# Late modulation columns summed on VectorE during the convolutions; decay weights in 33 small items with four buffers

## The chip, the cores and the metric

The kernel runs on one core of a Trainium2 chip. The metric is device time of one execution in microseconds; the kernel before has a median of 1655.15 over three runs (1654.78 to 1664.68). In this text PE is TensorE, PEld its weight load, DVE is VectorE, ACT is ScalarE, POOL is GpSimd and SP is SyncE.

## The reference, cut to what matters

One layer of a two-stream block in fp32: 1024 latent tokens and 256 context tokens, 1024 features. It modulates the inputs with columns computed from `c`, projects them to q, k, v, gates and decay rates, runs two linear-attention mixers, and ends with a projection and an MLP. These lines bear on the change:

```python
mod_x = (silu_c @ w_ada[l] + b_ada[l])[:, None, :]          # 6 * 1024 columns; shift/scale 1 are needed at once,
sh1x, sc1x, gt1x, sh2x, sc2x, gt2x = jnp.split(mod_x, 6, axis=-1)   # the other four parts only after the mixers
hx = rmsnorm(x, norm1_g[l]) * (1.0 + sc1x) + sh1x
p = h @ w_in                                                 # q_a, k_a, v_a, g_a, r_a, qkv_b, g_b, ...
lr = jnp.einsum('btr,zrk->zbtk', r_a, w_lr) + b_lr[:, None, None, :]
gla_log_a = (jax.nn.log_sigmoid(lr.astype(f32)) / GLA_TAU)   # summed along 64-token chunks, then exp
qkv = jax.nn.silu(short_conv(qkv_b, conv_w, rows)).astype(f32)
ya = rmsnorm(o_gla, gla_norm_g) * jax.nn.silu(p['gla_g'])    # the gates
```

## The kernel before, in words

The program is a row of phases: modulate (to 62 us), project (62 to 541 us), mix, merge and MLP. The change is in `project_phase` alone. Each engine there runs an instruction list of its own, written out in one fixed order, and waits on semaphores; nothing is planned at run time.

**Units and outputs.** `UNITS` lists 15 column groups of `w_in`, 256 columns each but for the first. Each is loaded by SP (`load_unit`), rounded by ACT and completed by DVE (`split`, lines 758 and 917: high and low part). PE forms each output as 8 x 3 matmuls (`mm3`, lines 80 to 82) in one of three PSUM buffers of `ps_main`; it may start output i only when ACT has copied out output i - 3 (`main_out`). All engines walk the same list `outs`:

- 3 small outputs, then 32 outputs of the convolution units k, k, v, v, q, q: two tiles per unit, each of three outputs (512, 512 and 256 tokens) for k and v, two for q. ACT copies them to the single buffer `u_sb`; after the last one DVE does the convolution (`conv`, lines 929 to 938), ACT the silu and the square, PE the sums of squares (`sums`, line 1157) one tile later, DVE the norm (955). PE also transposes k and v two tiles back (1176), and DVE copies that out (`turn_out`, 974), the first two groups before its convolution.
- 10 outputs ka and qa (ACT puts them into `qk`), 20 outputs va and 32 gate outputs. For these ACT copies each to `t_sb` (879), gates through Silu, and POOL (SP for the last unit) stores it.

**Decay rates.** Twelve outputs of kind `lr` stand in the same list, four behind qa, four in the first va unit, four at the end of the second: one small matmul (1191), then on ACT a copy and Abs, Exp, Ln (844 to 851), on DVE a min-and-subtract (1070), and after each four the running sums (`decay_sums`, scans of line 1006).

**Decay weights.** 17 items (`ITEMS`), four token tiles each (two for the context): DVE forms differences (`weight_sums`, 1017 or 1024 to 1027), ACT the exponential (`weight_exp`, 801 to 807), DVE multiplies by q or k (`weigh`, 1038), SP stores (`store_item`, 642). `SUMS_AT` and `WEIGH_AT` put an item's differences at one output and its product at the next, with the exponential at the first of the two; there are two buffers. 9 items start in the va outputs, 8 in the gate outputs. The Silu of the gates and the Exp of the items are in different function tables, so ACT loads a table at each turn (lines 750 and 879).

**Late modulation columns.** The four parts of `mod_x` that are needed later (32 groups of 128 columns) are made during the 32 gate outputs, one group behind each: SP loads 512 KB of `w_ada` (617), PE multiplies by silu(c) (`late_columns`, 1111), DVE copies the row out (`late_out`, 962), PE turns it into a column (`late_turn`, 1117).

## Time and profile before

| | us |
|---|---|
| median of three runs (lowest, highest) | 1655.15 (1654.78, 1664.68) |
| the profiled execution, its own time | 1664.6 |
| its span | 1662.8 |
| PE busy / DVE busy / ACT busy in the span | 1517.3 / 946.6 / 745.6 |
| mean granted TensorE clock | 0.961 |

The page cuts the span into 40 slices of 41.6 us. The phase that is changed covers slices 2 to 13:

```profile
PE   7699999998899697787888997899999999999997
DVE  4345451475540245555557439455555599988875
ACT  6446253546541444435434215455555554333333
PEclk9699999998999899999899999999999999999999
DMA  9313332355984466656614311244445586454322
```

A digit is a busy share in tenths (9 is 90% or more); PEclk is the clock that TensorE was granted, in tenths of full speed. A busy PE is not PE at its peak, since matmuls overlap and their ends are modelled: the distance from one start to the next says more than a duration.

### The profile page before, as it was taken

The numbers are of one execution on the slowest core, as the hardware profiler recorded it, in microseconds if no ns is written. First come the engines' busy times: TensorE is split into PE (matmuls) and PEld (weight loads), VectorE is DVE, ScalarE is ACT, GpSimd is POOL, SyncE is SP. The second block draws the span as 40 slices with busy tenths as digits, with TensorE's granted clock in tenths as the row PEclk, the third lists the DMA queues.
The fourth block names the chain that finished last, engine by engine and source line by source line (L and its number), as shares of the span: only waits on it lengthen the run. The fifth ranks groups of instructions, "written<-read, shape, count | busy, mean of one in ns | idle before, by whom it ended". The sixth has DMA issues, their size and how long they took to land. (4 is left out here: it accounts for less than half of the span.)

```text
span 1662.8 us, 33993 instructions
## 1 busy us (share of the span) xinstructions
PE 1517.3 (91%) x14508; PEld 1284.8 (77%) x14508; DVE 946.6 (57%) x1330; ACT 745.6 (45%) x1249; POOL 265.5 (16%) x237
## 2 busy tenths in 40 slices
PE   7699999998899697787888997899999999999997
PEld 6488878786798687776777886788888878888885
DVE  4345451475540245555557439455555599988875
ACT  6446253546541444435434215455555554333333
POOL 0001110011110132233223104132222200000000
PEclk9699999998999899999899999999999999999999
DMA  9313332355984466656614311244445586454322
GB/s 325 84 62 107 89 112 63 111 178 162 290 262 143 126 209 188 196 172 206 182 52 164 115 64 63 96 139 142 156 160 164 177 310 253 141 183 161 123 89 102
DMA packets 195736, 254.44 MB, mean 153 GB/s; under 512 B 34525, under 2 KB 127201, under 8 KB 195586
## 3 DMA queue, kind: packets, MB, share of 16 engines
q1 hardware_dynamic: 190002, 234.31, 43.4%
q0 software_dynamic: 5584, 17.95, 3.4%
q8 instruction: 116, 1.90, 0.5%
q14 instruction: 34, 0.28, 0.1%
HBM read 178.17 MB, written 74.05 MB: 152 GB/s over the span
## 5 line engine op out<-in xcount | busy, mean ns | idle before, releaser
L87 PE MATMUL fps<-xh_m,w1r_hi 128*128 128x512 f32 x448 | 176.6, 394 | 11.9 <-ACT s L2562 3.1
L88 PE MATMUL fps<-xl_m,w1r_hi 128*128 128x512 f32 x448 | 175.5, 392 | 0.0
L89 PE MATMUL fps<-xh_m,w1r_lo 128*128 128x512 f32 x448 | 175.3, 391 | 0.0
L87 PE MATMUL fps<-bh,ah 128*128 128x512 f32 x448 | 174.4, 389 | 0.4 <-DVE acc L2891 0.4
L88 PE MATMUL fps<-bl,ah 128*128 128x512 f32 x448 | 174.3, 389 | 0.0
L89 PE MATMUL fps<-bh,al 128*128 128x512 f32 x448 | 174.3, 389 | 0.0
L80 PE MATMUL ps_main<-whi,hhi 128*128 128x256 f32 x416 | 126.8, 305 | 6.5 <-ACT t_sb L879 4.0
L2534 ACT ACTIVATE ah<-araw 128x2048 fp32r<-128x2048 f32 x28 | 53.8, 1921 | 162.6 <-PE fps L89 133.6
L80 PE MATMUL ps_main<-hhi,whi 128*128 128x512 f32 (+1 forms) x336 | 125.6, 374 | 0.0
L81 PE MATMUL ps_main<-wlo,hhi 128*128 128x256 f32 x416 | 122.8, 295 | 0.0
L82 PE MATMUL ps_main<-whi,hlo 128*128 128x256 f32 x416 | 122.7, 295 | 0.0
L82 PE MATMUL ps_main<-hhi,wlo 128*128 128x512 f32 (+1 forms) x336 | 122.5, 364 | 0.0
L81 PE MATMUL ps_main<-hlo,whi 128*128 128x512 f32 (+1 forms) x336 | 122.4, 364 | 0.0
L87 PEld LDWEIGHTS fps<-xh_m,w1r_hi 128*128 128x128 f32 x448 | 84.7, 189 | 31.8 <-issue 8.6
L89 PEld LDWEIGHTS fps<-xh_m,w1r_lo 128*128 128x128 f32 x448 | 84.8, 189 | 17.8
L87 PEld LDWEIGHTS fps<-bh,ah 128*128 128x128 f32 x448 | 84.1, 188 | 18.8 <-issue 1.2
L88 PEld LDWEIGHTS fps<-xl_m,w1r_hi 128*128 128x128 f32 x448 | 85.0, 190 | 17.6
L89 PEld LDWEIGHTS fps<-bh,al 128*128 128x128 f32 x448 | 84.1, 188 | 17.5
L88 PEld LDWEIGHTS fps<-bl,ah 128*128 128x128 f32 x448 | 84.1, 188 | 17.3
L2736 DVE TENSOR_TENSOR w1r_lo<-w1raw,w1r_hi 128x512 fp32r<-128x512 f32 x96 | 75.9, 792 | 36.7 <-ACT w1r_hi L2525 36.7
L80 PEld LDWEIGHTS ps_main<-whi,hhi 128*128 128x128 f32 x416 | 85.1, 205 | 11.6 <-issue 11.6
L81 PEld LDWEIGHTS ps_main<-wlo,hhi 128*128 128x128 f32 x416 | 85.2, 205 | 0.0
(325 smaller groups left out, 3301.0 us busy)
## 6 DMA issues: line engine op xcount, KB each, us to landing
s_hid<-hb SPq DMA_DIRECT2D x112, 256.0 KB, 2.3
araw<-s_hid SPq DMA_DIRECT2D x28, 1024.0 KB, 5.6
room<-in_w_ada SPq DMA_DIRECT2D x32, 512.0 KB, 4.9
w1raw<-in_w_ff SPq DMA_DIRECT2D x16, 1024.0 KB, 5.7
w2b<-in_w_ff SPq DMA_DIRECT2D x16, 1024.0 KB, 9.8
raw<-in_w_in SPq DMA_DIRECT2D x14, 1024.0 KB, 5.3
s_wl<-room SPq DMA_DIRECT2D x24, 512.0 KB, 4.6
wl<-s_wl SPq DMA_DIRECT2D x16, 768.0 KB, 7.2
```

The costliest lines, as they stand in the source:

```text
L80: pe.matmul(out, lhi, rhi, start=start, stop=False)
L81: pe.matmul(out, lhi, rlo, start=False, stop=False)
L82: return pe.matmul(out, llo, rhi, start=False, stop=stop)
L87: pe.matmul(out, lhi, rhi, start=start, stop=False, skip_group_check=True)
L88: pe.matmul(out, lhi, rlo, start=False, stop=False, skip_group_check=True)
L89: return pe.matmul(out, llo, rhi, start=False, stop=stop, skip_group_check=True)
L2534: act.activation(flat(a_hi[v][:]), flat(araw[n % 2][:]), ACT.Copy).then_inc(a_hi_done, 1)
L2736: dve.tensor_tensor(w1r_lo[:, i], weight(n), w1r_hi[:, i].bitcast(F32), ALU.subtract).then_inc(w_lo, 1)
```

## The change

- The late columns leave the gate outputs and PE. `late_sum` on DVE multiplies and adds the eight 128-column pieces of a group (two `tensor_scalar`, six `scalar_tensor_tensor`, one addition), one group behind each of the 32 convolution outputs. `late_turn` stays on PE, as one matmul per group, against a column of ones; PE does them in batches ahead of `sums`, three groups behind. The loads of `w_ada` go to two buffers during the convolutions, issued by SP between the unit loads.
- The 12 rates are no outputs any more. They come two at a time behind the last three ka outputs and the first three qa outputs, in `ps_sq`, context first; Abs and the min read PSUM, so that the copy to `lr_x` is gone.
- The decay weights are 33 items of two token tiles: three around qa, then one at every 1.6 outputs of va and gate. Three buffers serve the first twelve, four the rest. Differences are at output n, the exponential at n + 1, and the product at the next item's start, behind its differences.
- Running sums of both halves of the latent tokens now have room at once (`cs_of`).

```diff
-        LRSEG = (0, 2, 1)
+        LRSEG = (2, 0, 1)
...
-        cs_lat, cs_ctx = room[:, 5120:7200], m.sb("cs_ctx", [P, 1040])[:]
-        slots = [room[:, 7200 + 2048 * i:9248 + 2048 * i] for i in range(2)]
+        cs_ctx = m.sb("cs_ctx", [P, 1040])[:]
+        cs_of = [room[:, 5120:7200], room[:, 7200:9280], cs_ctx]
...
+        slots = [room[:, 9280:10304], room[:, 10304:11328], lr_flat, room[:, 0:1024]]
...
+        NROW, LAG = 6, 3
+        arow = t_sb[:, 0:3].rearrange("p x (y n) -> p (x y) n", n=P)
+        brow = t_sb[:, 3].rearrange("p (x n) -> p x n", n=P)
+        late = [cs_ctx[:, :KT * P], lr_flat]
...
-                        if kind == "qa":
-                            outs.append((u, "lr", 2 * j + s, 0))
...
-                    if u == VA and t < 4:
-                        outs.append((u, "lr", 4 + t, 0))
-                    if u == VA + 1 and t >= 6:
-                        outs.append((u, "lr", 2 + t, 0))
...
-        PART = ((0, 4), (4, 4), (8, 2))
+        PART = ((0, 2), (2, 2), (4, 2), (6, 2), (8, 2))
+        CTX = 4
         KIN, QIN = LEVELS, LEVELS + 1
-        KINDS = [KIN, QIN] + list(range(LEVELS))
-        ITEMS = [(0, kind) for kind in KINDS] + [(2, KIN)] + [(1, kind) for kind in KINDS]
-        def place(n):
-
-            if n < 2 * NT:
-                return VA + n // NT, n % NT
-            return VA + 2 + (n - 2 * NT) // TL, (n - 2 * NT) % TL
-
-        starts = [1 + 2 * i for i in range(9)] + [20 + 2 * i for i in range(8)]
-        SUMS_AT = {place(n): i for i, n in enumerate(starts)}
-        WEIGH_AT = {place(n + 1): i for i, n in enumerate(starts)}
+        REST = [QIN] + list(range(LEVELS))
+        ITEMS = ([(CTX, KIN), (0, KIN), (1, KIN)] + [(x, kind) for x in (0, 1) for kind in REST]
+                 + [(x, kind) for x in (2, 3) for kind in [KIN] + REST])
+        SLOT = [i % 3 if i < 12 else i % 4 for i in range(len(ITEMS))]
+        uses = lambda i: SLOT[:i].count(SLOT[i])
+
+        def tick(u, kind, j, s):
+
+            if kind in ("ka", "qa"):
+                return 3 * j + s if kind == "ka" else 6 + 2 * j + s
+            if kind in ("va", "gate"):
+                return 10 + NT * (u - VA) + j if kind == "va" else 10 + 2 * NT + TL * (u - VA - 2) + j
+            return -1
+
+        starts = [6, 7, 8] + [10 + 8 * i // 5 for i in range(len(ITEMS) - 3)]
+        SUMS_AT = {n: i for i, n in enumerate(starts)}
+        EXP_AT = {n + 1: i for i, n in enumerate(starts)}
+        weighed = [n for n in starts[1:]] + [starts[-1] + 2]
+        conv_outs = [i for i, o in enumerate(outs) if o[1] in ("k", "v", "q")]
+        LATE_AT = {i: g for g, i in enumerate(conv_outs)}
+        GATE0 = 10 + 2 * NT
+
+        def rates_at(n):
+
+            return (2 * n - 6, 2 * n - 5) if 3 <= n < 9 else ()
...
             def load_late(g):
-                if g < NL:
-                    sp.wait_ge(wt_done, 8 if g < 2 else 9)
-                    sp.wait_ge(st_qk, 16)
-                else:
+                if g >= NL:
                     sp.wait_ge(ar_ready, g - NL + 1)
                 c0 = LATE0 + g * P
-                sp.dma_start(late[g % NL].rearrange("p (k n) -> p k n", n=P), av[:, :, c0:c0 + P]).then_inc(ld_a[g % NL], 16)
+                sp.dma_start(late[g % NL].rearrange("p (k n) -> p k n", n=P), av[:, :, c0:c0 + P]).then_inc(ld_a[g % 4], 16)
...
+            load_late(0)
+            load_late(1)
+            load_unit(3)
+            g = 2
+            for u in range(4, VA + 1):
                 load_unit(u)
-                if u == NU - 3:
-                    for i in range(4):
-                        store_item(i)
-                if u == NU - 2:
-                    for i in range(4, 8):
-                        store_item(i)
-                    load_late(0)
-                    load_late(1)
-                    store_item(8)
-                    load_late(2)
-            for g in range(NL, NLATE):
-                load_late(g)
-                if g % 2 == 0 and 9 <= 7 + g // 2 < len(ITEMS):
-                    store_item(7 + g // 2)
-                if g - 4 >= NLATE - TL:
-                    store_gate(g - 4 - NLATE + TL)
-            for t in range(TL - 4, TL):
+                upto = min(sum(o[0] <= u - 3 for o in outs) - 3 + NL, NLATE) if u < VA else NLATE
+                for g in range(g, upto):
+                    load_late(g)
+                g = upto
+            load_unit(VA + 1)
+            load_unit(VA + 2)
+            done = 0
+            for u, upto in ((VA + 3, 10), (VA + 4, 10 + NT), (VA + 5, GATE0)):
+                done = store_items(done, upto)
+                load_unit(u)
+            for t in range(TL):
+                done = store_items(done, GATE0 + 3 * TL + t)
                 store_gate(t)
+            for i in range(done, len(ITEMS)):
+                store_item(i)
             for i in range(4):
                 sp.wait_ge(st_g[i], 32)
-            for i in range(2):
-                sp.wait_ge(st_w[i], 32 * ((len(ITEMS) + 1 - i) // 2))
+            for i in range(4):
+                sp.wait_ge(st_w[i], 32 * SLOT.count(i))
...
+            def rates(j):
+                n, b = SEG[LRSEG[j // 4]][1], j % 2
+                log_exp()
+                if j == 0:
+                    act.wait_ge(ar_ready, NLATE)
+                act.wait_ge(lr_ready, j + 1)
+                if j >= 2:
+                    act.wait_ge(lr_done, j - 1)
+                act.activation(lr_e[:, b, :n], ps_sq[:, j % 3, :n], ACT.Abs).then_inc(lr_abs, 1)
+                act.wait_ge(lr_abs, j + 1)
+                act.activation(lr_e[:, b, :n], lr_e[:, b, :n], ACT.Exp, scale=-1.0).then_inc(lr_exp, 1)
+                act.wait_ge(lr_exp, j + 1)
+                act.activation(lr_e[:, b, :n], lr_e[:, b, :n], ACT.Ln, bias=1.0).then_inc(lr_ln, 1)
...
+                n = tick(u, kind, j, s)
+                for x in rates_at(n):
+                    rates(x)
+                if n in EXP_AT:
+                    weight_exp(EXP_AT[n])
...
-            def late_out(g):
-                dve.wait_ge(ar_ready, g + 1)
-                if g >= 2:
-                    dve.wait_ge(sel_done, g - 1)
-                dve.tensor_copy(arow[:, g % 2], ps_sq[:, 2 * (g % 2), :P]).then_inc(ar_out, 1)
+            def late_sum(g):
+                a, b, step = arow[:, g % NROW], brow[:, g % 2], ar_step[g % 2]
+                w = late[g % NL].rearrange("p (k n) -> p k n", n=P)
+                before = 8 * (g // 2)
+                dve.wait_ge(ld_a[g % 4], 16 * (g // 4 + 1))
+                if g >= NROW:
+                    dve.wait_ge(sel_done, g - NROW + 1)
+                for k in range(KT):
+                    to, c = (a, b)[k % 2], K.csil[:, k, 0:1]
+                    if k < 2:
+                        dve.tensor_scalar(to, w[:, k], c, None, ALU.mult).then_inc(step, 1)
+                    else:
+                        dve.wait_ge(step, before + k - 1)
+                        dve.scalar_tensor_tensor(to, w[:, k], c, to, ALU.mult, ALU.add).then_inc(step, 1)
+                dve.wait_ge(step, before + KT)
+                dve.tensor_tensor(a, a, b, ALU.add).then_inc(ar_ready, 1)
+
+            def late_kept():
+                dve.wait_ge(sel_done, NLATE)
+                dve.tensor_copy(K.mod[:, 32:40, 1], K.cols[:, 56:64])
+                dve.tensor_tensor(K.mod[:, 16:48, 0], ps_sq[:, 2, 256:256 + NLATE], K.cols[:, 16:48], ALU.add).then_inc(mod_done, 1)
...
+                n = tick(u, kind, j, s)
+                if n == 3:
+                    late_kept()
+                for x in rates_at(n):
+                    rates(x)
+                if n in SUMS_AT:
+                    weight_sums(SUMS_AT[n])
+                    if SUMS_AT[n]:
+                        weigh(SUMS_AT[n] - 1)
+                if i in LATE_AT:
+                    late_sum(LATE_AT[i])
                 if u >= 1 and i + 1 == out_by[u - 1] + 1 and u + 1 < NU:
                     split(u + 1)
-            dve.wait_ge(sel_done, NLATE)
-            dve.tensor_copy(K.mod[:, 32:40, 1], K.cols[:, 56:64])
-            dve.tensor_tensor(K.mod[:, 16:48, 0], ps_sq[:, 1, :NLATE], K.cols[:, 16:48], ALU.add)
+            weigh(len(ITEMS) - 1)
...
-            def late_columns(g):
-
-                pe.wait_ge(ld_a[g % NL], 16 * (g // NL + 1))
-                if g == 0:
+            def rates(j):
+                if j == 0:
+                    pe.wait_ge(rt_out, 3)
+                    pe.wait_ge(ld_s, 64)
                     pe.wait_ge(lnss_done, 8)
-                if g >= 2:
-                    pe.wait_ge(ar_out, g - 1)
-                w = late[g % NL].rearrange("p (k n) -> p k n", n=P)
-                for k in range(KT):
-                    q = slice(32 * (k % 4), 32 * (k % 4) + 32)
-                    last = pe.matmul(ps_sq[q, 2 * (g % 2), :P], K.csil[:, k, :], w[:, k, :], start=(k < 4), stop=(k >= 4))
-                last.then_inc(ar_ready, 1)
+                if j >= 3:
+                    pe.wait_ge(lr_done, j - 2)
+                if j == 0:
+                    late_turns(NLATE)
+                if j == 2:
+                    pe.wait_ge(mod_done, 1)
+                t0, n = SEG[LRSEG[j // 4]]
+                pe.matmul(ps_sq[:, j % 3, :n], wlr[:, j % 4 * P:(j % 4 + 1) * P], raT[0:RANK + 1, t0:t0 + n], start=True,
+                          stop=True).then_inc(lr_ready, 1)
 
             def late_turn(g):
 
-                pe.wait_ge(ar_out, g + 1)
-                pe.matmul(ps_sq[:, 1, g:g + 1], arow[:, g % 2], K.sel[:, 8:9], start=True, stop=True).then_inc(sel_done, 1)
+                pe.wait_ge(ar_ready, g + 1)
+                pe.matmul(ps_sq[:, 2, 256 + g:257 + g], arow[:, g % NROW], K.ones[:, 0:1], start=True, stop=True).then_inc(sel_done, 1)
+
+            turned = [0]
+
+            def late_turns(upto):
+
+                for g in range(turned[0], upto):
+                    late_turn(g)
+                turned[0] = max(turned[0], upto)
...
-                    if kind == "gate":
-                        g = (u - NU + 4) * TL + j
-                        late_columns(g)
-                        if g:
-                            late_turn(g - 1)
...
+                        if n_norm(cn - 1):
+                            pe.wait_ge(lnss_done, n_norm(cn - 1))
+                        late_turns(LATE_AT[i] - LAG + 1 if i in LATE_AT else NLATE - 1)
                         sums(cn - 1)
                     if kind in ("k", "v", "q") and s >= last_s - 1:
                         turn(cn - 2, (0, 1) if s < last_s else (2,))
-            late_turn(NLATE - 1)
+                    for x in rates_at(tick(u, kind, j, s)):
+                        rates(x)
```

## Rows read from the trace of the kernel before

**Rows 1.** four stages of the phase: start:end, then per engine busy us and count, clock, DMA

```profile
78.70:255.90 177.20, 177.20 (x897) 146.72 (x895) 83.30 (x111) 84.04 (x91) 21.40 (x26) 1.00 0.31 95
255.90:314.50 58.60, 58.11 (x267) 44.76 (x265) 12.21 (x15) 27.50 (x35) 2.17 (x3) 1.00 0.18 54
314.50:397.50 83.00, 73.88 (x501) 67.72 (x500) 55.36 (x100) 41.82 (x73) 12.12 (x22) 0.90 0.61 196
397.50:538.00 140.50, 128.24 (x1333) 117.33 (x1336) 56.48 (x88) 57.91 (x70) 13.55 (x25) 0.95 0.70 215
```

**Rows 2.** waits in the va stage: us in total, times, longest

```profile
ACT room L801 <- DVE room L1027: 28.7, 6, 6.2
PE ps_main L80 <- ACT t_sb L879: 4.0, 3, 2.9
```

**Rows 3.** PE timeline after such a wait: start us, duration us, engine, line, operation

```profile
328.67 0.41 PE L82 MATMUL ps_main<-whi,hlo 128*128 128x256 f32 x1
328.88 0.41 PE L80 MATMUL ps_main<-whi,hhi 128*128 128x256 f32 x1
```

**Rows 4.** PE timeline, first matmuls of two va outputs, then round one gate output

```profile
340.18 0.28 PE L80 MATMUL ps_main<-whi,hhi 128*128 128x256 f32 x1
343.06 0.28 PE L80 MATMUL ps_main<-whi,hhi 128*128 128x256 f32 x1
480.02 0.65 PE L1111 MATMUL ps_sq<-room,csil 128*32 128x128 f32 x16
480.59 0.38 PE L1117 MATMUL ps_sq<-sel,lr_x 128*128 128x1 f32 x2
480.84 0.36 PE L80 MATMUL ps_main<-whi,hhi 128*128 128x256 f32 x1
483.87 0.64 PE L1111 MATMUL ps_sq<-room,csil 128*32 128x128 f32 x16
```

**Rows 5.** PE's waits in the gate stage

```profile
PE ps_sq L1117 <- DVE lr_x L962: 8.8, 3, 3.9
PE ps_sq L1111 <- DMA room<-in_w_ada: 3.5, 1, 3.5
```

**Rows 6.** ACT timeline in the gate stage: one table turn, and an exponential of 1024

```profile
438.06 0.39 ACT L879 ACTIVATE t_sb<-ps_main 128x256 f32<-128x256 f32 x1 [2.40 <-PE ps_main L82]
438.47 1.28 ACT L750 ACT_TABLE_LOAD   x1
439.77 1.92 ACT L801 ACTIVATE room<-room 128x2048 f32<-128x2048 f32 x1
441.70 1.28 ACT L879 ACT_TABLE_LOAD   x1
408.52 1.06 ACT L806 ACTIVATE room<-room 128x1024 f32<-128x1024 f32 x1 [0.97 <-DVE room L1017]
```

**Rows 7.** groups by line and shape, PE: busy us, mean ns, idle before

```profile
L1191 PE MATMUL ps_main<-raT,wlr 17*128 17x512 f32 x16 | 8.9, 636 | 2.6 <-ACT t_sb L879 2.6
L1191 PE MATMUL ps_main<-raT,wlr 17*128 17x256 f32 x8 | 3.0, 452 | 0.0
```

**Rows 8.** DVE: four scalar_tensor_tensor of 128 columns in a row, and their group

```profile
572.16 1.12 DVE L1600 SCALAR_TENSOR_TENSOR rr<-pr,gt,vtn 128x128 f32<-128x128 f32 x4 [1.77 <-PE pr L1759]
L1600 DVE SCALAR_TENSOR_TENSOR rr<-pr,gt,vtn 128x128 f32<-128x128 f32 x80 | 22.5, 344 | 17.3 <-PE pr L1759 16.7 <-ACT vtn L1485 0.5
```

**Rows 9.** DVE timeline, one v tile of the convolutions

```profile
172.19 1.29 DVE L974 COPY room<-ps_tr 128x512 f32<-128x512 f32 x2 [4.97 <-PE ps_tr L1176]
175.85 0.89 DVE L929 TENSOR_SCALAR room<-room,cols 128x1280 f32<-128x1280 f32 x1 [2.37 <-ACT room L857]
180.30 0.42 DVE L974 COPY room<-ps_tr 128x256 f32<-128x256 f32 x1
190.71 0.89 DVE L929 TENSOR_SCALAR room<-room,cols 128x1280 f32<-128x1280 f32 x1 [2.37 <-ACT room L857]
```

**Rows 10.** the late columns' loads (line 617), issue to landing

```profile
DMA to landing us min/median/max: 3.8/4.9/9.7
```

More of the change, by code:

```diff
@@ L585, in item @@
             t0, n = PART[part]
-            return t0, n, kind, slots[i % 2][:, :512 * n], (cs_ctx if part == 2 else cs_lat), 4 * n
+            cs = cs_of[2 if part == CTX else part // 2]
+            off, z = (0, 8 * PW) if part == CTX else (8 * PW * (part % 2), 16 * PW)
+            return t0, n, kind, slots[SLOT[i]], cs, off, z
         def view(t, off, dims):
@@ L997, in _ @@
             last.then_inc(ab_kept, 1)
-            def decay_sums(part):
-                cs = cs_ctx if part == 2 else cs_lat
-                if part == 0:
-                    dve.wait_ge(init_done, 4)
-                dve.wait_ge(lr_done, (4, 12, 8)[part])
-                for x in range(4 * PART[part][1]):
-                    at = slice(2 * PW * x, 2 * PW * (x + 1))
-                    last = dve.tensor_tensor_scan(cs[:, at], restart[:], cs[:, at], 0.0, ALU.mult, ALU.add)
-                last.then_inc(cs_done, 1)
@@ new lines, in weight_sums @@
+            def weight_sums(i):
+                t0, n, kind, w, cs, off, z = item(i)
+                if uses(i):
+                    dve.wait_ge(st_w[SLOT[i]], 32 * uses(i))
+                elif SLOT[i] == 2:
+                    dve.wait_ge(lr_done, 12)
+                elif SLOT[i] == 3:
+                    dve.wait_ge(wt_done, 10)
+                    dve.wait_ge(st_qk, 16)
+                dve.wait_ge(cs_done, 1 if i == 0 else 2 if ITEMS[i][0] < 2 else 3)
+                ahead, past, half_ = off, off + z, 8 * C
@@ L1185, in _ @@
                     pe.wait_ge(main_out, i - 2)
-                if kind == "lr":
-                    if j == 0:
-                        pe.wait_ge(rt_out, 3)
-                        pe.wait_ge(ld_s, 64)
-                    t0, n = SEG[LRSEG[j // 4]]
-                    pe.matmul(ps_main[:, i % 3, :n], wlr[:, j % 4 * P:(j % 4 + 1) * P], raT[0:RANK + 1, t0:t0 + n], start=True,
-                              stop=True).then_inc(main_ready, 1)
-                elif kind == "small":
+                if kind == "small":
                     t0, n = SEG[s]
```

143 lines of the change are left out of this document (62 added, 81 removed).

## The prediction, made blind

> **What bounds the kernel now.** I first read the slices of the page for where PE is not full, then the busy time of four stages of the project phase, then each stage's waits, and last the timelines of single outputs. The stages are the 32 convolution outputs, ka and qa, va, and the gates [rows 1]; together 459.3 us. In the first two PE is full (177.2 of 177.2 and 58.1 of 58.6) at full clock, while DVE and ACT have half their time free (83.3 and 84.0 of 177.2). The other two are not full, and they hold work that isn't the projection. A va output that meets no wait takes 2.88 us from its first matmul to the next output's (340.18 to 343.06) [rows 4], so 20 could take 57.6, but the stage takes 83.0 [rows 1]. The reader should see why in the waits: ACT waits six times for DVE's differences, 28.7 us in all, since differences, exponential and product of an item follow one another, and what PE needs, ACT's copy of its PSUM buffer, stands behind the exponential; PE's own longest wait on it is 2.9 us [rows 2]. Behind such a wait a 256-column matmul comes every 0.21 us (328.67 to 328.88) and not every 0.12 (2.88 over 24): the granted clock of the stage is 0.90, a mixture of the levels 2.4 and 1.2 GHz, and here PE had stood idle just before it fell [rows 1, 3]. So a wait costs more than its length.
>
> A gate output takes 3.85 us (480.02 to 483.87) [rows 4], 32 of them 123, and the stage 140.5 [rows 1]; the rest is the start of the late columns, where PE waits 8.8 us for DVE and 3.5 for a load [rows 5], with the lower clock behind it. In the 3.85 us the projection has 2.88. The columns' sixteen half-matmuls go from 480.02 to 480.59, the turn from 480.59 to 480.84, and the remaining 0.15 is lost at the changes between them.
>
> **The change, part by part.** All is counted on PE, since PE sets the time of all four stages.
>
> *Gates.* Columns and turns leave: 32 x 2.88 = 92.2. What must hold is that ACT keeps up. A gate output with an item costs ACT a copy 0.41 (438.06 to 438.47), a table load 1.30 (438.47 to 439.77), an exponential of 1024 elements, 1.06 and a little more before a table load, 1.08, and a load back, 1.30: 4.09 us [rows 6]. An output without one costs 0.41. Items come every 1.6 outputs, 18 exponentials in the first 28 gate outputs, and three weight splits of the length of a 2048-element pass, 1.92 [rows 6]: 18 x 4.09 + 10 x 0.41 + 3 x 1.92 = 83.5 us of ACT against 28 x 2.88 = 80.6 of PE. ACT is the longer by 2.9, but it may lag two outputs behind (three PSUM buffers, 5.8 us), and the last four outputs have no item. Following lag by lag through the outputs, PE stops only round the second split, where two exponentials stand at neighbouring outputs: about 2 us in all. I take 92.2 + 2.0 + 0.3 at the end = 94.5, against 140.5. The bounds are 92.2 and, if ACT had no slack at all, 92.2 + 2.9 plus a fallen clock, some 100. The same elements go through DVE as before in twice as many instructions; its 56.5 us in this stage [rows 1] leave room for that, and since its differences now stand ahead of the product of the item before, ACT's input is ready when ACT comes. A store has half the bytes and four buffers, about 6.4 outputs or 18 us for differences, exponential, product and store. SP no longer waits for columns, so its stores go out as products finish. POOL's queue is unchanged.
>
> *va.* Twelve exponentials of half the size without table loads in 20 outputs, again a step behind the differences, and no rates on ACT: PE's waits and its low clock should go. 20 x 2.88 = 57.6, and 1.4 for the row transposes and changes: 59.0 against 83.0. The three buffers give 4.8 outputs, 13.8 us, for a cycle. DVE enters va late, since the last rates' running sums stand in front; I allow 1.5 us.
>
> *ka and qa.* Twelve rate matmuls instead of four stand here. For 512 tokens one costs 8.9 / 8 = 1.11 us, for 256 it costs 3.0 / 4 = 0.75 [rows 7]. Four of 512 move in, and four of 256: 7.4 us, 66.0 against 58.6. ACT has 27.5 of 58.6 busy [rows 1] and takes on eight more rates without their PSUM copy, spread two to an output of 5 us; nothing is late there by my count. The moved rates are also what va no longer carries.
>
> *Convolutions.* PE gets the 32 turns, 0.25 us each [rows 4]: 8.0 us on an engine without a gap. DVE gets 32 sums. Four `scalar_tensor_tensor` of 128 columns take 1.12 us, so one start follows the last by (1.12 - 0.344) / 3 = 0.26 [rows 8]; every sum step waits only for the step before the last, which 0.26 hides. One group is 8 x 0.26, the tail of the last 0.08, and an addition of at most 0.34: 2.5 us, 80 in all, on 83.3 busy of 177.2 [rows 1]. That fits in the sum, but the order decides: after its convolution DVE must do three sums before the next one, and there are two buffers. The third sum can only start when the buffer of the first has been read and loaded again, median 4.9 us from issue to landing [rows 10]. For a v tile: convolution and last copy 175.85 to 180.72 = 4.87, first sum 2.5, landing 4.9 (the second sum and at times a split lie beside it), third sum 2.5, the copy of the transposes 1.29 [rows 9, 10]: 16.06 us. PE's tile is 190.71 - 175.85 = 14.86, set by PE as DVE's wait of 2.37 shows [rows 9], and 15.61 with three turns. DVE is 0.45 late per tile; in k tiles both engines have more to do, and I count them alike: 8 x 0.45 = 3.6, of which the slack of the PSUM buffers eats a little: 3 us. The q tiles have two sums for two buffers and nothing to wait for. Bounds of a landing are 3.8 and 9.7 [rows 10]: at 3.8 no loss, at 9.7 8 x 5.25 = 42. I take the median, since most of the 32 lie near it and this stage has a DMA share of 0.31 against 0.70 where they were measured [rows 1]. SP issues some of these loads behind a unit load that waits for a split; by my count those have 8 us. Sum: 177.2 + 8.0 + 3.0 = 188.2.
>
> By the rows a next small DVE operation starts before the one in front has ended, 0.26 after its start against a duration of 0.344 [rows 8]. The Trainium skill ("VectorE: DVE Perf Modes", section "The DRAIN you can't avoid") says that the next operation does not start until the pipeline is empty; by that a group would be 8 x 0.344 + 0.34 = 3.1 us, a v tile 17.2, and the stage would lose 13 us and not 3. The row decides against it here.
>
> **The sum.** 188.2 + 66.0 + 59.0 + 94.5 + 1.5 = 409.2 against 459.3: 50 us less. The profiled execution was 1664.6 and would be 1614.6. The median of the three runs lies 9.5 below it, and I take the same 50 off: 1605.
>
> **The rivals.**
>
> *B, loads late in the convolutions.* DVE becomes the bound of eight tiles. For it: the cycle above is already even with PE's at the median landing. Against it: the free DMA queues [rows 1]. At a landing of 7.5 us a tile is 18.7, 3.1 too long, 24 us in all: 1605 + 21 = 1626.
>
> *C, ACT out of time in the gates.* For it: 83.5 against 80.6, and 18 turns of the tables where there were 8. If ACT had to wait for the differences of each item, four operations of some 0.35, it would lose 1.4 x 18 = 25 us: 1630. Against it: the differences no longer wait for ACT.
>
> *D, slower.* If landings are near the longest seen, 9.7, PE stops 5.25 us in each of eight tiles, and, as in va, runs at half clock behind each stop: an output's worth of time, 2.88, is lost again [rows 3, 4, 10]. 8 x (5.25 + 2.88) = 65 against a gain of 53 without convolution waits: 1655 + 12 = 1667. It decides from a landing of about 8.2 us on.
>
> *E, a table turn that costs twice.* If each load held ACT for 2.6 us and not 1.3, 36 loads would add 47 us to ACT in the gates: no gain there, 1650. For it stands nothing in the rows: copy and exponential start 1.30 after the load's start [rows 6]. The Trainium skill ("ScalarE: Activation LUTs", section "What ACT_TABLE_LOAD costs") gives 1283 ns and a drain of 1380 ns behind it for every switch; the first agrees with 1.28 here, the second is not seen.
>
> **How the numbers follow.** The forecast has a chance of 0.63, B 0.17, C 0.13, D 0.04, E 0.03. Within 1% (16.6 us) is what a measurement of this kernel cannot tell from no change. The forecast is all faster; of B, C and E 0.06 lie within 1%; D is 0.04: faster 0.90, same 0.06, slower 0.04. The best case has no waits at all and turns at half price in a batch: 50 + 3 + 2 + 1.5 + 4 = 60 less, 1595. Upwards the range takes in B and C at their prices and a little of both: 1633. Outside are D, E and the tail of B with C.
>
> **What would show it.** Gate outputs 2.88 us apart and a gate stage of 94 to 96; va near 59 at full clock; 4.1 us of ACT for a gate copy with its item; sums of 2.5 us on DVE; convolutions near 188, with PE's waits there under 5 us in all. If the convolutions take 200 or more, the landings were mis-sized; if gates take over 100 with PE waiting on the copy to `t_sb`, ACT was; if va keeps a clock of 0.9, the waits have only moved.

## The result and the profile after

The changed kernel has a median of 1608.97 us over four runs (1606.56 to 1618.1), beside 1656.1 over four of the kernel before: a ratio of 0.9715, with an interval of 0.9664 to 0.9766. A second series gave 0.9721 (0.9697 to 0.9745). The prediction was 1605, 50 us less than before; measured are 47 less (1656.1 to 1608.97). The profiled execution took 1618.1 with a span of 1616.3, where 1614.6 was forecast for it. The mean granted clock went from 0.961 to 0.970, PE's busy time from 1517.3 to 1478.0, DVE's from 946.6 to 1016.5.

The four stages of the phase, after, cut at the same outputs as in [rows 1] (start:end, length, then busy us and count of PE, PE's weight loads, DVE, ACT and POOL, the granted clock, the DMA share and GB/s):

```profile
78.50:272.30 193.80, 186.72 (x953) 155.16 (x952) 152.96 (x391) 84.69 (x91) 21.34 (x26) 0.98 0.61 173
272.30:336.90 64.60, 64.60 (x289) 48.58 (x287) 33.13 (x80) 39.65 (x61) 1.97 (x3) 1.00 0.18 57
336.90:394.90 58.00, 58.00 (x486) 58.00 (x486) 42.17 (x95) 25.55 (x49) 12.53 (x22) 1.00 0.70 235
394.90:487.20 92.30, 92.27 (x769) 92.07 (x768) 48.75 (x77) 83.61 (x94) 13.43 (x25) 1.00 0.49 167
```

Read down the lengths: va and gates are now full and at full clock, 25.0 and 48.2 us shorter than in [rows 1]; ka and qa, which now hold all twelve rates, are 6.0 longer; the convolutions are 16.6 longer, and they are the one stage where PE isn't full (186.72 of 193.80) and the clock not 1.00. Together 408.7 against 459.3: 50.6 less. Each gate output starts 2.88 us after the one before; first matmuls of two neighbours in the timeline of PE:

```profile
394.85 0.28 PE L80 MATMUL ps_main<-whi,hhi 128*128 128x256 f32 x1
397.73 0.28 PE L80 MATMUL ps_main<-whi,hhi 128*128 128x256 f32 x1
```

What is lost in the convolutions is in the waits. First PE's, then two of DVE's, of the convolution stage after (us in total, times, longest):

```profile
PE ps_tr L1229 <- DVE room L1014: 7.1, 4, 3.8
```

```profile
DVE t_sb L992 <- DMA cs_ctx<-in_w_ada: 15.6, 7, 5.1
DVE t_sb L992 <- DMA lr_e<-in_w_ada: 2.7, 2, 2.4
```

PE waits four times for DVE's copy of the transposes, and DVE nine times for a late load. Both ends of the link can be seen on DVE's timeline round one tile (start, duration, engine, line, operation, count; in brackets the idle time before and its releaser):

```profile
133.97 0.47 DVE L992 TENSOR_SCALAR t_sb<-cs_ctx,csil 128x128 f32<-128x128 f32 x2
134.35 1.66 DVE L995 SCALAR_TENSOR_TENSOR t_sb<-cs_ctx,csil,t_sb 128x128 f32<-128x128 f32 x6
136.05 0.29 DVE L997 TENSOR_TENSOR t_sb<-t_sb 128x128 f32<-128x128 f32 x1
136.26 0.47 DVE L992 TENSOR_SCALAR t_sb<-lr_e,csil 128x128 f32<-128x128 f32 x2
...
143.51 0.48 DVE L992 TENSOR_SCALAR t_sb<-cs_ctx,csil 128x128 f32<-128x128 f32 x2 [4.88 <-DMA cs_ctx<-in_w_ada]
...
145.81 0.68 DVE L1014 COPY room<-ps_tr 128x512 f32<-128x512 f32 x1
```

A group takes 136.26 - 133.97 = 2.29 us. Two follow each other, then the third has to wait 4.88 us for the buffer that the first had read until about 136.0, and behind the third stands the copy of the transposes that PE needs. Where the next tile is late as well, PE stops, and runs at half clock for a while. PE's timeline at its longest stop:

```profile
185.05 0.66 PE L1229 MATMUL ps_tr<-ident,room 128*128 128x128 f32 x2 [3.76 <-DVE room L1014]
...
186.79 0.63 PE L80 MATMUL ps_main<-hhi,whi 128*128 128x512 f32 x1
187.22 0.63 PE L81 MATMUL ps_main<-hlo,whi 128*128 128x512 f32 x1
...
190.48 0.40 PE L80 MATMUL ps_main<-hhi,whi 128*128 128x512 f32 x1
190.71 0.40 PE L81 MATMUL ps_main<-hlo,whi 128*128 128x512 f32 x1
```

After the stop a 512-column matmul comes every 0.43 us, the spacing of the lower of the clock's two levels (1.2 GHz), and every 0.23, that of 2.4 GHz, again from 190.5 on; the whole output took 7.85 where one of its kind takes 5.55. The page gives the median from issue to landing of the two buffers' loads (512 KB each):

```profile
cs_ctx<-in_w_ada SPq DMA_DIRECT2D x16, 512.0 KB, 5.9
lr_e<-in_w_ada SPq DMA_DIRECT2D x16, 512.0 KB, 5.5
```

### The profile page after: what moved, and what is told of

Read it like the earlier page. It is cut to its first block and busy times, and to the rows that moved or that the text cites. A ratio compares the mean times of both kernels' runs of the same rounds, so it can differ in the third digit from the quotient of the medians.

```text
span 1616.3 us, 33365 instructions
## 1 busy us (share of the span) xinstructions
PE 1478.0 (91%) x13996; PEld 1259.6 (78%) x13996; DVE 1016.5 (63%) x1654; ACT 766.6 (47%) x1277; POOL 265.7 (16%) x237
## 5 line engine op out<-in xcount | busy, mean ns | idle before, releaser
L80 PE MATMUL ps_main<-whi,hhi 128*128 128x256 f32 x416 | 117.9, 284 | 0.0
L81 PE MATMUL ps_main<-wlo,hhi 128*128 128x256 f32 x416 | 117.8, 283 | 0.0
L82 PE MATMUL ps_main<-whi,hlo 128*128 128x256 f32 x416 | 117.8, 283 | 0.0
L1624 DVE COPY_PREDICATED gdn_zz<-lev_m,pd 128x256 f32<-128x256 uint32 x120 | 47.4, 441 | 63.7 <-PE pd L1794 60.8
L2936 DVE TENSOR_TENSOR acc<-acc,fps 128x1024 f32<-128x1024 f32 x54 | 64.7, 1218 | 29.1 <-PE fps L89 29.1
```

The costliest lines, as they stand in the source:

```text
L80: pe.matmul(out, lhi, rhi, start=start, stop=False)
L81: pe.matmul(out, lhi, rlo, start=False, stop=False)
L82: return pe.matmul(out, llo, rhi, start=False, stop=stop)
L1624: dve.copy_predicated(zz[:, lev, b], lev_m[:, b, lev].bitcast(mybir.dt.uint32).unsqueeze(1).broadcast_to([P, NH, C]), cells(pd[b])).then_i ...
L2936: dve.tensor_tensor(to, to, got, ALU.add).then_inc(o_out, 1)
```

## The experiments

The theory was: the gain is two changes that work on different stages, the late columns' move (convolutions and gates) and the small items (va and gates, and ka and qa by the rates); what the convolutions lose beyond the turns is the landing of the loads with only two buffers; and the items need both their number of buffers and their order. The rivals: one of the two parts brings all of it; the convolutions lose by DVE's amount of work, whatever the buffers; three buffers, or the order, would have done nothing.

### late_only: the late columns' move alone

The kernel before with the sums on DVE in the convolutions, and the loads with them. Items, rates and their order stay.

```diff
-                if kind == "gate":
-                    late_out((u - NU + 4) * TL + j)
+                if i in LATE_AT:
+                    late_sum(LATE_AT[i])
```

> The kernel before with one half of the change: late columns summed on VectorE during the convolutions, rates and the 17 large decay items as before. My theory (the two halves act on different stages, and large items in step still bind): convolutions as in the changed kernel, 194 us; ka and qa 59; va 83 as before; gates 100 to 105, since an item's chain of differences 2.4, exponential 1.95 and product 2.2 is 6.6 us where two gate outputs take 5.8. Sum 438, 21 us under the kernel before: about 1635. Rival 1 (the late columns were all there was to gain, small items add nothing): about 1609, gates at 92. Rival 2 (the items bind the gates, taking columns off TensorE only uncovers them): gates stay above 125, the time is that of before or worse.

Measured: 1657.25 (ratio 0.9974, 0.9951 to 0.9997), where I had expected 1635. The gates:

```profile
415.26:525.34 110.08, 97.44 (x769) 96.35 (x768) 48.86 (x59) 56.87 (x69) 13.44 (x25) 0.95 0.39 128
```

PE's largest wait from va on, and ACT's:

```profile
PE ps_main L80 <- ACT t_sb L887: 16.5, 9, 4.9
ACT room L805 <- DVE room L1046: 41.0, 12, 6.1
```

The gates go from 140.5 to 110.1 and not to 92, nor to the 100 to 105 on record: with the columns gone, PE meets what stood behind them, ACT's copy behind exponentials of 2048 elements that wait for their differences. The convolutions take 194.1, as in the full change, va 82.9, as before. The phase gains 13.7 us and the median only 3.6; what the profiles say of the rest is below.

### items_only: the small items alone

The changed kernel with the late columns put back behind the gate outputs on PE, in two buffers; the items take three instead of four, since the fourth is now a late buffer. This half holds four things at once: small items, the step between differences and exponential, the third buffer, and the rates' move out of va.

```diff
-        late = [cs_ctx[:, :KT * P], lr_flat]
+        late = [room[:, :KT * P], cs_ctx[:, :KT * P]]
...
-                if i in LATE_AT:
-                    late_sum(LATE_AT[i])
+                if kind == "gate":
+                    late_out((u - NU + 4) * TL + j)
```

> The changed kernel with the other half alone: the late columns go back to TensorE, one group behind each gate output (two load buffers, the decay items keep three). My theory: convolutions 177, ka and qa 64 to 65, va 58 at full clock, gates 32 x 3.85 = 123 and a few us at the start: 425, 34 us under the kernel before, about 1622. With late_only's 21 the two gains would add to 55, a little above the 47 measured together. Rival (small items cost VectorE and ScalarE so much that they only pay when TensorE does not wait on VectorE for the columns): va above 65 or gates above 135, time above 1640.

Measured: 1666.46 (ratio 1.0042, 1.0026 to 1.0059). 1622 was expected. Convolutions 177.1 and va 58.0: va's 25 us come from this half of the change alone. How much of them is the items and how much the eight rates that left va was not separated; the rates' matmuls cost ka and qa 6.0 us where they went, and in va PE had also waited 5.1 us round them (2.6 before a rate's matmul, 2.5 for a rate's copy). But the gates grew to 159.2. PE's waits in the gates:

```profile
PE ps_sq L1147 <- DMA room<-in_w_ada: 13.0, 5, 4.0
PE ps_sq L1147 <- DMA cs_ctx<-in_w_ada: 11.2, 3, 5.6
```

The timeline before the longest of them tells why the load is late (a store of an item is at L656, a late load at L631):

```profile
445.61 0.64 PE L1147 MATMUL ps_sq<-cs_ctx,csil 128*32 128x128 f32 x16
449.76 0.88 SPq L656 DMA_DIRECT2D s_wl<-lr_e  x2
450.69 0.55 SPq L631 DMA_DIRECT2D cs_ctx<-in_w_ada  x1
458.98 1.08 PE L1147 MATMUL ps_sq<-cs_ctx,csil 128*32 128x128 f32 x16 [5.59 <-DMA cs_ctx<-in_w_ada]
```

PE had read `cs_ctx` by 446.3, but its next load was issued at 450.69 only, right behind a store that had to wait until DVE had its product at 449.74. A store of a product that isn't ready stands ahead of a load whose buffer is free. So this kernel shows the items' effect on va cleanly, and on the gates only together with a worse queue.

### items_three: the same with a third late buffer, loads ahead of stores

```diff
-        late = [room[:, :KT * P], cs_ctx[:, :KT * P]]
+        late = [room[:, :KT * P], cs_ctx[:, :KT * P], room[:, KT * P:2 * KT * P]]
```

In SP's list a late load now stands ahead of the stores of its output.

> items_only with a third load buffer for the late columns in the gates, and with each load issued ahead of the stores of decay items on SyncE's queue. Theory (items_only's gates, 159 us and not 126, come from loads issued late behind a store that waits for its product, 24 us of waits for loads with half clock behind each): gates 124 to 130, project phase 32 us under the kernel before, time about 1632; then the two halves of the change add up. Rival (the loads are late because the small stores fill the queues): gates above 145, time above 1650.

Measured: 1638.98 (ratio 0.9882, 0.9861 to 0.9904), gates 133.3. The third late buffer and the loads' place in the queue gave 159.2 - 133.3 = 25.9 us together; which of the two gave how much was not tested. The 124 to 130 on record were too low: the gates still miss the 32 x 3.85 = 123 of the rows by 10, of which 8.2 are two waits for a load. (The items have three buffers here and not four; three_three shows that this costs nothing where the late columns are in the convolutions, and it was not tried here.) The items' half is thus worth 26.3 us in the phase (459.3 to 433.0), the late columns alone 13.7, both 50.6. The whole is 10.6 more than its parts. A likely reason is that the move takes PE's work from the gates, but the gates can use that only when ACT no longer stands in the way, as it does in late_only.

### late_three: a third buffer for the late loads

```diff
-        late = [cs_ctx[:, :KT * P], lr_flat]
+        late = [cs_ctx[:, :KT * P], lr_flat, K.gt2[:]]
```

`K.gt2` is memory that only the later phases write; the sums are the same work in the same places.

> The changed kernel with a third load buffer for the late columns (in a tensor that is unused during the convolutions). Theory (the four stops of TensorE in the convolutions, 7.1 us, and one output at half clock behind the longest, 2.3 us, come from VectorE waiting for the load of the third sum of a tile): VectorE's 18 us of waits for these loads nearly vanish, convolutions 184 to 186 instead of 194, 8 to 9 us less than the changed kernel in the same call. Rival (VectorE's own work, with sums of 2.3 us, is what fills a tile): waits for transposes' copies stay, time as the changed kernel.

Measured: 1601.19 (1598.32 to 1604.53), ratio 0.9645 (0.9620 to 0.9669), below the changed kernel's 0.9721 (0.9697 to 0.9745). The convolution stage, and DVE's only wait for a late load in it:

```profile
76.20:259.90 183.70, 183.46 (x955) 153.23 (x953) 152.73 (x391) 84.64 (x91) 21.35 (x26) 1.00 0.65 183
```

```profile
DVE t_sb L992 <- DMA gt<-in_w_ada: 0.5, 1, 0.5
```

193.8 became 183.7 with the same 153 us on DVE: the loss of 10.1 was the landing, not the amount of work. What is left over 177.2 is 6.5 us; PE has 0.24 us of waits in the stage, so nearly all of it is the 32 turns, at 0.20 each. The other stages are unchanged (64.6, 58.0, 92.2).

### late_one: a single buffer

```diff
-        late = [cs_ctx[:, :KT * P], lr_flat]
+        late = [cs_ctx[:, :KT * P]]
...
-            load_late(1)
             load_unit(3)
-            g = 2
+            g = 1
```

> The changed kernel with one load buffer for the late columns instead of two: each sum's load can only start when the sum before it has ended. This is case D of the prediction, made to happen. With landings of 5.9 us, two of three in a tile lie bare on VectorE: 6.2 + 3 x 2.3 + 2 x 5.9 = 24.9 us for a v tile, 26.3 for a k tile, where TensorE needs 15.5 and 17.7; q tiles 16 against 13. Theory 1 (VectorE is then the bound, and TensorE's half clock behind each stop is hidden in the next wait): convolutions 177 + 4 x 9.4 + 4 x 8.6 + 4 x 3 = 261, time about 1677. Theory 2 (as the prediction priced D, the half clock adds some 2.9 us at each of eight tiles): 284, time about 1700. Rival (the loads hide anyway): 194.

Measured: 1691.29 (ratio 1.0188, 1.0135 to 1.0242): 1.9% slower than before. The convolutions:

```profile
77.76:342.32 264.56, 201.86 (x954) 165.16 (x953) 147.98 (x373) 84.95 (x91) 21.40 (x26) 0.87 0.43 123
```

and PE's and DVE's largest waits in them:

```profile
PE ps_tr L1228 <- DVE room L1013: 55.5, 8, 14.2
DVE t_sb L991 <- DMA cs_ctx<-in_w_ada: 102.3, 19, 7.2
```

The 264.6 is near the 261 that DVE's work and the landings alone ask for, and far from the 284 with half clock on top. Against three buffers the convolutions lose 80.9 us, of which 62.7 are waits of PE (7.2 more, on ACT, beside these 55.5); the other 18.2 are PE's matmuls at a mean granted clock of 0.87. But these 18.2 are no price on top: DVE waits 102.3 us for loads and never for the copy of an output ahead of a convolution, so DVE's cycle sets the time, and what PE loses by its clock it waits less. Three, two and one buffer do the same work and give 183.7, 193.8 and 264.6; the single one costs ka and qa 9.7 us more as well (74.3), with 7.6 of PE's waits there. This is the prediction's rival D in kind, landings that nothing covers eat the whole gain; its extra term, 2.88 us of half clock at every stop, isn't seen.

### in_step: the exponential at the same output as its differences

```diff
-        EXP_AT = {n + 1: i for i, n in enumerate(starts)}
+        EXP_AT = {n: i for i, n in enumerate(starts)}
...
-                    weight_sums(SUMS_AT[n])
                     if SUMS_AT[n]:
                         weigh(SUMS_AT[n] - 1)
+                    weight_sums(SUMS_AT[n])
```

> The changed kernel with the offset undone: an item's exponential stands at the output of its differences, and the product of the item before ahead of the differences. Same items, same buffers. My theory (case C of the prediction): ScalarE waits for four differences of about 0.35 us at each item, some 1.4 us x 18 in the gates, where it has no slack: gates 92 to about 112, va unchanged, time about 1630. Rival (small items and more buffers do it all, the order is of no matter): gates stay at 92, time as the changed kernel.

Measured: 1622.11 (ratio 0.9770, 0.9748 to 0.9793), about 8 us above the changed kernel by the ratios (0.0049 of 1660); the stages 193.9, 66.2, 65.0 and 93.9. So the offset is worth 1.6 in the gates, where I had expected 20 (and rival C had 25), and 8.6 in ka, qa and va, where I had expected nothing. The longest of PE's waits from ka on is early in va:

```profile
PE ps_main L80 <- ACT room L888: 4.5, 1, 4.5
```

and ACT's timeline at it, where the copies for PE (L888, and L902 after it) stand behind the exponential (L839):

```profile
347.31 0.63 ACT L839 ACTIVATE lr_e<-lr_e 128x512 f32<-128x512 f32 x1 [7.80 <-DVE lr_e L1078]
...
348.36 0.58 ACT L888 ACTIVATE room<-ps_main 128x512 f32<-128x512 f32 x1
```

The differences came late because DVE had the last running sums (5.23 us of scans) in front. In the gates a table load of 1.28 us stands between a copy and its exponential, and covers most of what the differences take: ACT waits for them four times there, 5.1 us in all.

### two_slots: small items with two buffers

```diff
-        SLOT = [i % 3 if i < 12 else i % 4 for i in range(len(ITEMS))]
+        SLOT = [i % 2 for i in range(len(ITEMS))]
```

> The changed kernel with two buffers for the decay items instead of three and then four. A buffer's round is differences 1.4, the wait for its exponential's turn and table 2 to 3, exponential 1.1, product 1.2, store 3: 9 to 10 us, and with two buffers it may take 3.2 outputs, 9.2 us. Theory (buffers beyond two only buy slack): va 58 to 62, gates 93 to 100, time 1610 to 1618. Rival (the stores are the point, without three buffers VectorE waits for each landing): gates above 105, time above 1625.

Measured: 1644.1 (ratio 0.9922, 0.9892 to 0.9953); va 70.6, gates 109.7, together 30.0 more than after. DVE's largest wait from ka to the gates' end, and PE's:

```profile
DVE room L1084 <- DMA s_wl<-room: 48.4, 17, 5.3
```

```profile
PE ps_main L80 <- ACT t_sb L902: 22.6, 14, 3.0
```

The theory on record (buffers beyond two buy only slack, 1610 to 1618) was wrong, and its rival right: an item's store has to land before the next differences can be written; DVE waits for that, ACT for DVE, and PE for ACT. PE's waits of 22.6 us go with a loss of 30.0.

### large_apart: large items, out of step

late_only's kernel with the exponential one output behind the differences, and each product behind the next item's differences; 17 items and two buffers as before.

```diff
+        EXP_AT = {place(n + 1): i for i, n in enumerate(starts)}
```

> late_only with the offset alone added: still 17 large items, two buffers and the rates in their old places, but an item's exponential stands one output behind its differences, and its product behind the differences of the next. Per two gate outputs (5.76 us) ScalarE has 5.3 and VectorE 4.6. Theory (the order is what binds late_only's gates, 110 us with stops at nearly every item): gates 93 to 97, va 76 to 83 since its stops come from the rates too, time about 18 us under late_only, 1640. Rival (a 2048-element item is too long a piece between two copies, whatever the order): gates above 104, time as late_only.

Measured: 1668.09 (ratio 1.0053, 1.0030 to 1.0076), worse than late_only where I expected a gain: va 90.7 against 82.9, gates 115.1 against 110.1. ACT's largest wait from va on, and DVE's:

```profile
ACT room L806 <- DVE room L1047: 58.9, 12, 9.0
```

```profile
DVE room L1044 <- DMA s_wl<-room: 34.3, 8, 6.8
```

The offset makes an item hold its buffer longer, so with two the differences wait for a store to land, and ACT for them; in late_only DVE's waits for stores from va on are 3.4 us in all. Out of step helps only where there are buffers enough. Large items with three buffers were not tried, so whether the items had to be small, or only needed more buffers, stays open.

### three_three: three late buffers, three for the items

```diff
-        late = [cs_ctx[:, :KT * P], lr_flat]
+        late = [cs_ctx[:, :KT * P], lr_flat, K.gt2[:]]
...
-        SLOT = [i % 3 if i < 12 else i % 4 for i in range(len(ITEMS))]
+        SLOT = [i % 3 for i in range(len(ITEMS))]
```

> late_three (third load buffer for the late columns) with three buffers for the decay items throughout, without the fourth. A buffer then comes round every 4.8 outputs, 13.8 us in the gates, for differences, exponential, product and a store of 2.5 us, about 10 us. Theory (a turn in two_slots, 9.2 us, was too short for 10; three is long enough, the fourth is spare): va 58, gates 92 to 94, time as late_three, about 1601 to 1603. Rival (buffers count one by one): gates 98 or more.

Measured: 1602.77 (1598.04 to 1606.22), ratio 0.9648 (0.9617 to 0.9679), the same as late_three, and its stages are too (table below; gates 92.2). The fourth item buffer brings nothing that can be seen; the step that counts is from two to three.

### changed_again: the changed kernel once more

It has no edit.

> The changed kernel itself once more, beside the next three. Both theories of the project phase expect its stages as in its first profile, 193.8, 64.6, 58.0 and 92.3 us, and a ratio to the kernel before of 0.968 to 0.975. The mix phase is what this look is for: it took 332 us in the kernel before, 339 in the first profile of the changed one, 344 in late_only. If it comes out elsewhere between 330 and 345 here, it varies by itself; if at 339 again, the change carries something into it.

Measured: 1612.92 against 1659.79, ratio 0.9721 (0.9697 to 0.9745); stages 194.1, 64.6, 58.0 and 92.2, as in the first profile to 0.3 us. PE's wait in the convolutions is another, though:

```profile
PE ps_tr L1229 <- DVE room L1014: 8.3, 4, 3.7
```

Six profiles of kernels with two late buffers (this one, the first, late_only, in_step, two_slots, large_apart) have 6.4 to 8.3 us of such waits and stages of 193.5 to 194.1: the stage doesn't follow PE's waits. The expectation above asked for the mix phase as well; its answer is in the section on the prediction.

All stages in one table, in us, cut at the same outputs:

| kernel | conv. | ka, qa | va | gates | sum | ratio to before |
|---|---|---|---|---|---|---|
| before | 177.2 | 58.6 | 83.0 | 140.5 | 459.3 | 1 |
| after | 193.8 | 64.6 | 58.0 | 92.3 | 408.7 | 0.9715 |
| late_only | 194.1 | 58.5 | 82.9 | 110.1 | 445.6 | 0.9974 |
| items_only | 177.1 | 64.6 | 58.0 | 159.2 | 458.9 | 1.0042 |
| items_three | 177.1 | 64.6 | 58.0 | 133.3 | 433.0 | 0.9882 |
| late_three | 183.7 | 64.6 | 58.0 | 92.2 | 398.5 | 0.9645 |
| late_one | 264.6 | 74.3 | 58.0 | 92.2 | 489.1 | 1.0188 |
| in_step | 193.9 | 66.2 | 65.0 | 93.9 | 419.0 | 0.9770 |
| two_slots | 193.8 | 64.6 | 70.6 | 109.7 | 438.7 | 0.9922 |
| large_apart | 193.5 | 58.5 | 90.7 | 115.1 | 457.8 | 1.0053 |
| three_three | 183.7 | 64.5 | 58.0 | 92.2 | 398.4 | 0.9648 |

The best version is late_three, or three_three, some 12 us below the changed kernel by the ratios (0.0075 of 1660; each was timed against the kernel before, not against the other).

## Why the prediction was right, step by step

**Gates, 94.5 forecast, 92.3 measured.** The count of ACT was right: one turn of the tables is copy, load, exponential, load, and takes 431.02 - 426.95 = 4.07 us where 4.09 was summed:

```profile
426.95 0.38 ACT L902 ACTIVATE t_sb<-ps_main 128x256 f32<-128x256 f32 x1
427.36 1.28 ACT L769 ACT_TABLE_LOAD   x1
428.65 1.06 ACT L834 ACTIVATE room<-room 128x1024 f32<-128x1024 f32 x1
429.73 1.28 ACT L902 ACT_TABLE_LOAD   x1
431.02 0.66 ACT L902 ACTIVATE t_sb<-ps_main 128x256 f32<-128x256 f32 x2
```

ACT was busy 83.61 us in the stage (the forecast's 83.5 was for its first 28 outputs, and would be 85.1 with the last four), and three PSUM buffers carried its lag everywhere: PE has no wait here, so the 2 us of stops round a split didn't come. Rival E is out by the same rows, which put each operation 1.29 us behind the start of its table load; no drain of 1380 ns behind it, as the Trainium skill ("ScalarE: Activation LUTs", "What ACT_TABLE_LOAD costs") has it, is seen.

**va, 59.0 and an allowance of 1.5, measured 58.0.** 20 x 2.88 = 57.6 and 0.4 beside. The running sums in front did make DVE late, but the offset took that up: in_step shows a stop of 4.5 us at this place, where the allowance was 1.5. Here, not in the gates, is where rival C's mechanism lives.

**ka and qa, 66.0 forecast, 64.6 measured.** The eight extra rates cost 6.0 and not 7.4. They were priced at 8.9 / 8 and 3.0 / 4 of busy time [rows 7]. The groups of PE by line and shape after (busy us, mean ns) have less for the same twelve rates:

```profile
L1156 PE MATMUL ps_sq<-raT,wlr 17*128 17x512 f32 x16 | 7.9, 613 | 0.0
L1156 PE MATMUL ps_sq<-raT,wlr 17*128 17x256 f32 x8 | 2.3, 400 | 0.0
```

With 7.9 / 8 and 2.3 / 4 the eight would be 6.3. What is new is that two rates stand in a row; that they overlap more for it is my reading, and no run tried it.

**Convolutions, 188.2 forecast, 193.8 measured.** Here a size was off, in both terms, on opposite sides. The turns cost 0.20 and not 0.25: 6.5 for 8.0. The waits cost 10.1 for 3: 7.1 in four stops, 2.3 in one output at half clock, and some 0.7 of lesser slowness. The mechanism was the one named, a third sum that waits for the buffer of the first. The mis-sized term is the landing: 5.9 and 5.5 us against the 4.9 taken from the gates of before. I had argued that it might even be shorter, from the stage's DMA share of 0.31 [rows 1]. That is the share before the change; with the loads in it, it is 0.61. But the share of a stage isn't what decides either: the 4.9 were measured at 0.70, and late in those gates, from 484 to 530 us, the share is 0.59 and the median landing 4.1. What differs is what is in flight with a load. Late in the gates of before no item is left to be stored and a group comes every 3.85 us, so a load of 4.1 meets little more than the end of the one before. In the convolutions two sums follow each other, and so do the two loads that they release. Here is such a pair, and then its landings and that of a single load issued at 145.92:

```profile
136.37 0.54 SPq L629 DMA_DIRECT2D cs_ctx<-in_w_ada  x1
138.66 0.54 SPq L629 DMA_DIRECT2D lr_e<-in_w_ada  x1
```

```profile
DMA to landing us min/median/max: 6.4/6.8/7.1
DMA to landing us min/median/max: 3.9/3.9/3.9
```

The load of 136.37, with stores of k in flight beside it, is the one that DVE waits for until 143.51 in the lines above. The loads in front of the four stops took 7.1, 6.8, 7.4 and 5.3 us.

Put the medians, 5.9 for the landing, groups of 2.29 and turns of 0.20, into the prediction's sum for a v tile, and it is 16.06 + 1.0 - 0.42 = 16.64 against 15.46, 1.18 late, 9.4 for eight tiles, near the 10.1. But that is a mean over what happened: the four stops are behind the last k tile and behind three of the four v tiles, and one of them is 3.76 long. Half clock was used for rival D and left out of the forecast's own term, and the sum comes near without it, as it did in late_one. At the one slow output it may have counted: DVE waited 2.0 us for PE behind it.

**The DRAIN rule.** Six `scalar_tensor_tensor` of 128 columns take 1.66 us, which is (1.66 - 0.344) / 5 = 0.26 from start to start, as the rows of before said [rows 8], though each waits for a semaphore of the last but one. The Trainium skill's rule ("VectorE: DVE Perf Modes", "The DRAIN you can't avoid"), as the prediction read it, would have made a group 3.1 us; it is 2.29. The same section adds "A next op that is not held starts earlier", which the prediction left out, and with which the 0.26 agrees. The group of 2.5 was 0.21 too high: the addition starts at the forecast's 2.08, and the next group 136.26 - 136.05 = 0.21 us behind it, where a tail and an addition were priced at 0.42.

**The rivals.** B was in part what happened, at 5.3 to 7.4 in front of the four stops against its 7.5 at all eight tiles: the forecast and B are one mechanism at two sizes. D's landings of 9.7 didn't occur, and late_one, made to be D, came out without its term for half clock. C's price of 25 us in the gates was 1.6 in in_step; E is out, as said. The signs of the sum's errors were mixed (-2.2, -2.5, -1.4, +5.6), so 409.2 met 408.7 by some luck.

**From the stages to the median.** 50.6 us less in the phase gave 46.5 less span and 47.1 less median. Most of the difference is in the mix phase, whose code is the same. From its first to its last DVE operation it took 317.4 before, 323.9 after and 321.8 in changed_again, the same kernel once more; 314.5 in late_three and 318.6 in three_three; 328.9 in late_only, 314.6 in items_only and 326.9 in two_slots. In the profiles, late_only's 13.7 are eaten by these 11.5 us and by smaller differences elsewhere, and its mean granted clock in the phase is 0.91 against 0.94 before; but its profile was taken of the slowest of its ten executions, so this doesn't explain a median. Two profiles of one kernel differ by 2.1 us here, two kernels with the same four stages by 4.1, so a part is variation of single executions, and the changed kernel was some 5 us above before both times. Whether the rest comes from where the work starts or from the clock wasn't settled: none of the edits touched the mix phase. The argument on the four stages doesn't rest on it, but the 1605 does: it took the phase's 50 us off the median one for one.

## What to carry to other kernels

When work moves into a stage, price its loads by what will be in flight with each of them there, not by a median from another stage, and count the buffers so that the landing lies beside two other groups: here the third buffer cost no time anywhere and gave back 10 us, and the second was the difference between a gain of 3% and a loss of 2%. An engine that two others wait on needs buffers enough and its producers a step ahead, in this order: without the third buffer 30 of the phase's 50.6 us were lost (two_slots), without the step 10 (in_step), and the step without the buffers was a loss of its own (large_apart). And when two engines pace each other, ask which of them sets the cycle before adding up PE's waits and its half clock: in late_one they were two parts of one loss.

## What the runs showed of the hardware

- **A load lands later with others in flight.** In one stage of the changed kernel a 512 KB load alone took 3.9 us from issue to landing, and two issued 2.29 us apart, with stores beside them, 6.4 and 7.1. The medians of the same loads are 4.4 with one late buffer, 5.9 and 5.5 with two, and 6.7, 6.5 and 5.3 with three, where they cost next to nothing, being covered.
- **Waits and half clock go together.** PE's waits of 62.7 us in late_one go with a loss of 80.9, 22.6 in two_slots with 30.0, 7.1 after with 10.1 and 8.3 in changed_again with 10.4. Behind a stop a matmul of 512 columns comes every 0.43 us for some output or part of it, then every 0.23. Where another engine sets the cycle, as in late_one, this is no extra price.
- **A turn of one column** costs PE 6.5 / 32 = 0.20 us in batches; alone in a gate output of before it took 0.25 [rows 4].
